# The second block's output projection with seven products in place of eight

## The reference

```
mix   = gate_att * (att @ w_att_out) + gate_conv * (conv @ w_conv_out)   # 512 x 1024
x_mid = x + g1 * (mix @ w_o)                                             # w_o: 1024 x 1024
h2    = modulate(rmsnorm(x_mid, norm_ffn), sh2, sc2)
x     = x_mid + g2 * moe(h2)      # top group of 4, top 2 of its 8 experts, 32 experts in all
out   = rmsnorm(x, final_norm)
```

## Time and profile before

| | |
|---|---|
| median of three runs | 1892.02 us |
| profiled execution, its own time | 1900.21 us |
| its span, first to last instruction | 1898.6 us |
| PE busy | 1732.2 us (91%) |
| VectorE, ScalarE, GpSimd busy | 958.8, 513.1, 398.9 us |
| granted TensorE clock, mean | 0.958 |
| moved by DMA | 380.03 MB, mean 200 GB/s |
| costliest group: expert products L3947 | 361.8 us in 1504 instructions |

### The profile page before, as it was taken

The page is one execution under the profiler, slowest core; times in us unless marked ns, Lnnn a source line. Parts: engine busy times, 40 slices in busy tenths (PEclk is TensorE's granted clock), DMA queues, the critical chain, the costliest instruction groups (busy, mean ns, idle before and its releaser), DMA issues. The chain is left out here.

```text
span 1898.6 us, 29839 instructions
## 1 busy us (share of the span) xinstructions
PE 1732.2 (91%) x12382; PEld 1156.2 (61%) x12382; DVE 958.8 (50%) x1605; ACT 513.1 (27%) x973; POOL 398.9 (21%) x404
## 2 busy tenths in 40 slices
PE   7999988789999999899999998999979988978887
PEld 3554487778788888788888887744443323323332
DVE  1775885557488888823588888633130010000113
ACT  4223553341355545201211112620031011110101
POOL 0000017600588887400111110100010000000000
PEclk9999999999999999899999999999979989989998
DMA  9453034213432222322584323205389999999994
GB/s 356 177 208 124 17 89 100 56 38 144 155 124 81 86 89 90 114 92 91 187 326 157 116 89 106 78 31 224 131 313 419 426 426 425 426 426 426 425 422 197
DMA packets 80537, 380.03 MB, mean 200 GB/s; under 512 B 34464, under 2 KB 37536, under 8 KB 54672
## 3 DMA queue, kind: packets, MB, share of 16 engines
q1 hardware_dynamic: 70000, 350.03, 47.6%
q0 software_dynamic: 7104, 26.68, 3.8%
q10 hardware_dynamic: 3296, 1.38, 0.3%
HBM read 364.09 MB, written 19.92 MB: 202 GB/s over the span
## 5 line engine op out<-in xcount | busy, mean ns | idle before, releaser
L3947 PE MATMUL psum<-mem 128*64 128x512 f32 x1504 | 361.8, 638 | 23.2 <-DMA mem<-in_w_upe 10.4
L2091 PE MATMUL psum<-mem 128*128 128x256 f32 x1232 | 268.8, 380 | 3.8 <-ACT mem L378 2.7
L3947 PEld LDWEIGHTS psum<-mem 128*64 128x64 f32 x1504 | 116.0, 146 | 249.1 <-issue 242.4
L2091 PEld LDWEIGHTS psum<-mem 128*128 128x128 f32 x1232 | 233.5, 190 | 39.2 <-ACT mem L378 3.2
L3053 PE MATMUL psum<-mem 128*128 128x256 f32 x896 | 196.7, 381 | 3.3 <-DVE mem L3234 2.8
L3053 PEld LDWEIGHTS psum<-mem 128*128 128x128 f32 x896 | 169.9, 190 | 30.0 <-issue 5.3
L2201 DVE SCALAR_TENSOR_TENSOR psum<-mem,psum 128x512 f32<-128x512 f32 x220 | 150.2, 746 | 0.0
L1681 PE MATMUL psum<-mem 128*128 128x256 f32 x616 | 138.1, 384 | 5.2 <-issue 4.6
L1681 PEld LDWEIGHTS psum<-mem 128*128 128x128 f32 x616 | 117.4, 192 | 24.3 <-issue 7.0
L4018 DVE TENSOR_TENSOR mem<-mem,psum 128x512 f32<-128x512 f32 x16 | 11.0, 688 | 234.9 <-issue 202.9
L2048 POOL TENSOR_TENSOR mem<-mem 128x512 f32<-128x512 f32 x88 | 111.6, 1280 | 56.8 <-ACT mem L2071 56.8
(11 more groups left out here) (443 smaller groups left out, 2589.8 us busy)
## 6 DMA issues: line engine op xcount, KB each, us to landing
mem<-in_w_upe SPq DMA_DIRECT2D x30, 2048.0 KB, 25.4
mem<-in_w_gate SPq DMA_DIRECT2D x29, 2048.0 KB, 27.4
mem<-in_w_downe SPq DMA_DIRECT2D x27, 2048.0 KB, 31.7
mem<-in_ada SPq DMA_DIRECT2D x32, 1024.0 KB, 6.8
mem<-in_w_up SPq DMA_DIRECT2D x22, 1024.0 KB, 4.9
mem<-in_ada POOLq DMA_DIRECT2D x16, 1024.0 KB, 7.2
mem<-in_w_in_g SPq DMA_DIRECT2D x12, 1024.0 KB, 5.2
mem<-in_w_down SPq DMA_DIRECT2D x16, 704.0 KB, 4.0
```

The source lines that it names most:

```text
L2091: ins = pe.matmul(bank, w[:, i], rhs[:, i], start=first and i == 0, stop=last and i == self.N - 1, skip_group_check=True)
L3947: last = pe.matmul(bank[halves[h], :], xs[:, kt, halves[h]], pair[h][0][:, kt, cols], start=kt == 0, stop=kt == tiles - 1, skip_group_chec ...
```

## The change

```diff
+class SevenOut:
+    X, V, Z = (0, 1), (2, 3), 6
...
+    def weight_sums(self, pool, p):
+        self.make_s1(pool, p)
+        self.make_s2(pool, p)
+        self.make_s3(pool, p)
+        self.make_s4(pool, p)
...
+    def make_t2(self, dve, i, made):
+        dve.wait_ge(made, self.N + i + 1)
+        dve.wait_ge(self.t1_made, i + 1)
+        dve.tensor_tensor(self.t2[:, i], self.b22[:, i], self.t1[:, i], SUB).then_inc(self.t2_made, 1)
...
+    def product(self, pe, bank, w, rhs, first, last, done):
+        for i in range(self.N):
+            ins = pe.matmul(self.bank(bank), w[:, i], rhs[:, i], start=first and i == 0, stop=last and i == self.N - 1, skip_group_check=True)
+        ins.then_inc(done, 1)
...
+    def do_p7(self, pe, p):
+        pe.wait_ge(self.s3_made, p + 1)
+        pe.wait_ge(self.t3_made, self.N)
+        pe.wait_ge(self.u_added, p + 1)
+        self.product(pe, self.X[p % 2], self.quarter(p, 1, 0), self.t3, False, False, self.p7)
...
     def sync(sp):
         k.send_weights(sp)
         sp.dma_start(w_router.rearrange("p k n -> p (k n)"), k.d["w_router"]).then_inc(s["router"], 16)
-        experts.send(sp, 0, 6)
-        sp.wait_ge(r.summed, KD)
-        experts.send(sp, 6, 8)
+        experts.send(sp, 0, 4)
+        sp.wait_ge(r.p3, r.PAIRS)
+        experts.send(sp, 4, 8)
+
+    def gpsimd(pool):
+        for p in range(2, r.PAIRS):
+            r.weight_sums(pool, p)
...
+        r.do_p1(pe, 0)
+        r.do_p2(pe, 0)
+        for p in range(r.PAIRS):
+            if p == 0:
+                r.do_p5(pe, p)
+                spread_gate(0)
+                r.do_p6(pe, p)
+            else:
+                r.do_p6(pe, p)
+                r.do_p3(pe, p - 1)
+                r.do_p5(pe, p)
+            if p == 1:
+                spread_gate(1)
+                pe.wait_ge(s["router_gained"], 1)
+            r.do_p7(pe, p)
+            if p:
+                logits(2 * p - 2)
+                norm.sum(pe, 2 * p - 2)
+                norm.sum(pe, 2 * p - 1)
+            if p + 1 < r.PAIRS:
+                r.do_p1(pe, p + 1)
...
+            r.do_p4(pe, p)
+            if p + 1 < r.PAIRS:
+                r.do_p2(pe, p + 1)
+        r.do_p3(pe, r.PAIRS - 1)
         logits(KD - 2)
+        norm.sum(pe, KD - 2)
         norm.sum(pe, KD - 1)
...
+        @block.gpsimd
+        def _(pool):
+            for p in range(2):
+                out.weight_sums(pool, p)
...
                 dve.tensor_tensor(mix[:, m], gate_a[:, m], gate_b[:, m], ADD).then_inc(s["mix"], 1)
+                if m < out.N:
+                    out.make_t1(dve, m, s["mix"])
+                else:
+                    out.make_t2(dve, m - out.N, s["mix"])
+                    out.make_t3(dve, m - out.N)
+                    out.make_t4(dve, m - out.N)
...
-        self.slots = [k.at(at + 4096 * i, 4096) for i in range(7)] + [
+        self.slots = [k.at(at + 4096 * i, 4096) for i in (2, 3, 4, 5, 0, 1, 6)] + [
```

More of the change, by code:

```diff
@@ L2457, in mix_out_stage, with w_o_part @@
     return r
-OutputPart = collections.namedtuple("OutputPart", "sync tensor scalar vector summed root_turned logits gate_row normed")
-def w_o_part(k, mix, gate, x, x4, norm, gains, shift, expert_gate, gate_row, w_router, work, r_root, experts):
-    r = Residual(k, "w_o", 1, halves(k, "w_o"), mix, gate, lambda m: x[:, m], x4)
+OutputPart = collections.namedtuple("OutputPart", "sync gpsimd tensor scalar vector summed root_turned logits gate_row normed")
+def w_o_part(k, r, x4, norm, gains, shift, expert_gate, gate_row, w_router, work, r_root, experts):
     s = {n: k.sem("w_o_" + n) for n in ("router", "gains", "shifted", "shift_sum", "router_gained", "shift_mm", "bias", "diagonal", "gate_mm", "gate_row",
@@ L2529, in scalar @@
         for m in range(KD):
[L2530 to L2533, removed]
+            if m < 2:
+                act.wait_ge(s["gate_mm"], m + 1)
+                act.activation(gate_row[:, 512 * m:512 * m + 512], gate_bank[:, :], ACT.Copy).then_inc(s["gate_row"], 1)
+            r.row_done(act, m)
             norm.square(act, m, x4[:, m])
@@ L2541, in vector @@
             dve.tensor_scalar(diagonal[:, kt], k.c("ident"), expert_gate(kt), None, MUL).then_inc(s["diagonal"], 1)
+        r.add_a(dve, 0)
+        r.add_z(dve, 0)
         dve.wait_ge(s["router"], 16)
@@ L2547, in vector @@
         dve.tensor_reduce(shift_sum.rearrange("p (n o) -> p n o", o=1), shifted.rearrange("p k n -> p n k"), AX, ADD).then_inc(s["shift_sum"], 1)
-        for m in range(KD):
-            r.addition(dve, m)
-            if m == 4:
+        for p in range(r.PAIRS):
+            r.add_u(dve, p)
+            if p:
+                r.add_v12(dve, p - 1)
+            r.add_v(dve, p)
+            r.add_v22(dve, p)
+            if p + 1 < r.PAIRS:
+                r.add_a(dve, p + 1)
+            r.add_x(dve, p)
+            if p + 1 < r.PAIRS:
+                r.add_z(dve, p + 1)
+            if p == 2:
                 dve.wait_ge(s["shift_mm"], 1)
                 dve.tensor_tensor(bias, bias, gate_bank[:, 0:36], ADD).then_inc(s["bias"], 1)
+        r.add_v12(dve, r.PAIRS - 1)
         dve.wait_ge(s["logit_mm"], 1)
@@ L4082, in _ @@
         def _(pool):
+            out.gpsimd(pool)
             route.gpsimd(pool)
@@ L4239, in block_two @@
     x4 = three(6144, KD, SEQ)
-    merge_stage(k, att, conv, ga, gb, mix, Norm(k, "layer_norm", 6144, k.bank[4], k.bank[6], tiles=KC), k.at(7424, P))
-    k.frees_later([k.number("w_o", g) for g in range(4)], "w_o_summed", 2)
+    seven = SevenOut(k, "w_o", mix, lambda m: m2[:, 16 + m, 0:1], x, x4, 10240, 13312)
+    merge_stage(k, att, conv, ga, gb, mix, seven, Norm(k, "layer_norm", 6144, k.bank[4], k.bank[6], tiles=KC), k.at(7424, P))
     experts = Experts(k, 10240)
@@ L4254, in block_two @@
     r_root, shift = k.small[:, 56:60], m2[:, 24:32, 0]
-    out = w_o_part(k, mix, lambda m: m2[:, 16 + m, 0:1], x, x4, norm_ffn, gains, shift, lambda m: m2[:, 40 + m, 0:1], gate_row, w_router, 4724, r_root,
+    out = w_o_part(k, seven, x4, norm_ffn, gains, shift, lambda m: m2[:, 40 + m, 0:1], gate_row, w_router, 4724, r_root,
                    experts)
```

126 lines of the change are left out of this document (117 added, 9 removed).

## The result

The changed kernel is slower: over 22 runs of each (medians 1896.3 us before, 1905.1 after), the ratio to the kernel before is 1.0045, 95% interval 1.0031 to 1.0060, that is 8.5 us (5.9 to 11.4). The forecast was +2 us, with a range that ended at 1.0042.

What follows compares the result with a forecast made beforehand. The prediction took the kernel's end to be set by when the expert weight stream starts, hanging on turn 0's gather. Terms -4.9 + 5.4 + 1.0 + 0.5 gave +2.0 us, from 1892.0 to about 1894 us, range 1886.5 to 1900.

Steps and rivals of the forecast that it cites:

- The products: Output projection: 224 instructions of 256 columns replace 128 of 512, 50.2 us busy instead of 56.9, -6.7 us.
- the one wait on an addition: Output projection: only p7 of pair 0, right behind p6, waits for VectorE's addition, +0.7 us.
- The merge stage's end: Last block's sums t2, t3 and t4 on VectorE have no cover and delay TensorE's start, +1.1 us.
- Forecast to T0: Up to the end of the output projection's last product: 1.1 - 6.7 + 0.7 = -4.9 us.
- GpSimd's sums: Merge stage and projection: added 128x512 sums finish in time and cost nothing; upper bound +3 us if they block VectorE.
- Gather 0: Turn 0's gather: row stores held behind four loads delay its issue, +5.4 us, and the ninth slot's load its landing, +1.0.
- That the gather is what counts: Expert turns: the end is set by when the weight stream starts to be fed, which hangs on turn 0's gather.
- The clock in the gate product: Turn 0's gate product: TensorE's longer idle time keeps the low clock a little longer, +0.5 us, between 0 and 3.
- All of it from T0 to the last down product: Behind the output projection's last product: later gather issue +5.4, slower landing +1.0, low clock +0.5 us.
- The first rival: Row stores are not held behind the loads, so only -4.9 us is left: 1887 us, chance 0.15.
- The third: Rival: the projection doesn't shrink because hand-offs to VectorE aren't covered, +7.7 us: about 1902 us, chance 0.05.
- The second: Rival: gather waits for all of the ninth load (+4.9), low clock through the gate product (+3.0): 1900.5 us, chance 0.17.

Runs made afterwards that it cites:

- e12: e6 with the last tile's t2, t3 and t4 sums moved from the merge stage's end to the projection's start; ratio 1.0001 to the kernel before.
- e7: Changed kernel with three of the five late expert loads sent only once gather 0 has landed; ratio 1.0063 to the kernel before.
- e2: Kernel before with only the slots' part: four expert loads at the projection's start, four at its end; ratio 1.0052.
- e16: Kernel before with 48 small products, never run, inside the overflow turns' code; ratio 1.0005.
- e6: Changed kernel with the ninth slot loaded after the third pair, two loads ahead of the row stores and one behind them; ratio 0.9991 to the kernel before.
- e15: e12 with 48 small products, never run, inside the overflow turns' code; ratio 0.9957 to the kernel before.
- e14: e12 with 16 small products, never run, inside the overflow turns' code; ratio 0.9952 to the kernel before.
- e4: Changed kernel sending two loads, all four row stores, then three loads behind the last product; ratio 1.0037 to the kernel before.

## Why the prediction was wrong

The forecast of +2.0 us went wrong by two terms that it put at nothing: the clock behind the longer pause at the merge stage's end (+1.7) and the tail (+2.1). With them the profiles give +5.1; why the comparisons stand above that stays open. The large term, a later gather because the stores are held, had the right mechanism and about the right size. By its own steps, sizes within the profiles against those forecast:

- **The products, -6.7.** Right. e12's projection, at full clock, took 57.15 us against 63.63: -6.5 with the one wait on an addition (0.8 there, 0.7 in the changed kernel; forecast 0.7) and everything else in it. No other product waited for an addition.
- **The merge stage's end, +1.1.** The sums cost just that; the step that failed is that nothing followed from it. The longer pause brought the low clock into the projection's start, +1.7. Forecast to T0: -4.9; measured -3.8 (in all four profiles each) because 1.7 was missing and the rest was 0.6 better.
- **GpSimd's sums**, nothing: right, though VectorE and GpSimd did meet. In the merge stage of every changed profile two of VectorE's sums of t1 took 1.4 to 1.5 us in place of 0.42 and one addition into `mix` 1.6 to 1.7 in place of 0.69, 21 to 26 us ahead of its end; the stage got no longer than by the last sums. In e12 a sum with two SBUF inputs (L2742) took 1.64 us beside GpSimd's L2244 where its twin L2739 took 0.69, again without cost. The Trainium skill, SBUF — State Buffer, "SBUF: two separate sides", has a VectorE instruction with two SBUF inputs and a GpSimd one exclude each other for the whole instruction, and the trace agrees.
- **Gather 0.** The mechanism was right and the term mis-sized: the memset came 30.3 us behind the last product instead of 28.0, gather 0 at 31.45 instead of 29.5 (+7.4 against +5.4). The first store landed at 24.9 us and the last 5.4 us later. The forecast reckoned 10.5 MB at 425 GB/s; up to gather 0 the DMA moved 393 GB/s, and some 1.4 MB of the ninth load had moved before the last store was through. The landing took 5.0 us instead of 5.3. Together +7.9 to +8.0 for the first turn's rows, against +6.4.
- **That the gather is what counts** held only in part. e7 shows that an early gather with the loads behind it is worst of all. The step "the end is set by when the stream starts to be fed" should have been: by the bytes moved when it becomes full.
- **The clock in the gate product, +0.5.** It was nothing: the first 64 gate and up instructions took 16.80 us against 16.94.
- **All of it from T0 to the last down product, +6.9.** Measured +6.8. That so good a fit came out is partly luck: gather 0 was 1.6 us later than forecast, the clock cost 0.5 less, and about 1 us came back in the weight stream in a way that the account by bytes (+7.8) doesn't explain.
- **The tail** was not in the forecast: +2.1, of which 1.2 is the longer pause at the jump.

Inside the profiles this makes -3.8 + 6.8 + 2.1 = +5.1 us. The comparisons say 8.5 (5.9 to 11.4) and 6.3 (3.4 to 9.3), so 1 to 3 us are in no stretch that was read (the second interval still holds 5.1). The cause is open. In e12 the comparison is 4.4 us above the sum of its stretches (611.0 + 34.4 against 649.6), but so it is by 3 us in e2 and 4 in e16, which have the products and TensorE's order of before, while e6 and e15 are within 2 us and e14 is 2 us below. Code that never runs moved the time by 8 to 9 us between e12 and e14 or e15, of which their tails show 4 to 5, so where the code lies may be the cause of the rest as well; that is argued, not shown, since the stretch ahead of the merge stage varies by 9 us between profiles and hides it.

The first rival (stores not held) is refuted by the 18.8 us of the first store. The third is refuted by the one wait. The second had the size by other parts than it named: gather 0 waited only 0.7 us longer beside the ninth load, and the low clock hit the projection's start and the tail, not the gate product.

The Trainium skill, DMA: Bandwidth & Descriptors, "Queues, rings and completion order", has the engines take turns between queues, a packet at a time. e4's trace agrees: 161 packets of the gathers' queue beside 166 of SP's. What the prediction drew from it, that a gather hardly waits for SP's loads and that 15.6 us don't look like even turns, left out the size of the packets: with 4 KB against 16 KB, equal turns are what made it 11.6 us in e4. In the changed kernel the ninth load was nearly over, and the gather took 5.0 us, between the forecast's two prices (4.3 and 5.3).

## What to carry to other kernels

A transfer that the next stage needs must not stand behind bulk loads on the same queue: order the queue by what is due first, and use times in which DMA is idle, since bytes moved out of such a time are paid for in full once DMA is the bound. On a queue of its own it still shares the engines with the loads, packet by packet, and small packets get the small share (e4). A microsecond more of pause at a barrier can cost more than itself in TensorE's clock, so look at the granted clock behind each pause that a change makes longer. Before a difference of half a per cent is put down to a change's mechanism, move code that never runs and see whether the time moves with it.

## What was not expected of the hardware

- 16 products of 8 columns in a branch that is not taken moved the kernel from 1.0001 to 0.9952 of before; 48 of them did nothing to the kernel before (1.0005). The visible part is TensorE's pause at the jump: 2.3 to 2.8 us before, 2.9 to 4.7 with the change, 0.3 and 0.6 with the change and dead code. The packets of instructions on DMA queues q8 and q14 go along with it: 100 and 37 in before, e2 and e16, 102 and 38 with the change, 101 and 39 in e14 and e15. That the pause is the loading of code was not shown.
- A pause of 2.98 us at the barrier lowered TensorE's clock in eight of eight profiles, one of 1.84 us in none of ten; it cost 1.7 us. At the jump in the tail, pauses of 2.64 to 3.47 us left the clock up in three profiles.
- A store of 512 KB took 18.8 us behind four loads of 2 MB on SP's queue, against 3.4 us behind no load.
- A gather of 512 KB took 11.6 us beside loads of 2 MB, at one of its 4 KB packets for each 16 KB packet of the loads.
